# Key factors, directions and the bonus's sums multiplied beside the rates, four and four Fourier steps, four bonus products

## The reference, cut to what matters

```python
w_lora = w0 + einsum("btdr,drc->btdc", tanh(wd), w2)
decay = exp(-exp(-softplus(-w_lora) - 0.5))
a = sigmoid(a0 + einsum("btdr,drc->btdc", ad, a2))      # the rates
kk = normalised(k * k_k)                                # per head of 64
kd = k[:, :, None] * (1 + (a - 1) * k_a)                # key factors, for each direction
bonus = einsum("bthn,btdhn,hn->bth", r, kd, r_k)[..., None] * v    # sums over both directions d
y = fft2(u_fourier, axes=(1, 3)).real                   # the Fourier branch, whose projection is done here too
```

## Time and profile before

| | |
|---|---|
| time, median of 3 runs | 1986.52 us |
| the three runs | 1979.35, 1986.52, 1986.55 us |
| the profiled execution's own time | 1988.64 us |
| its span | 1986.8 us |
| mean granted TensorE clock | 0.953 of full speed |

### The profile page before, as it was taken

The page is one execution under the profiler, slowest core; times in us unless marked ns, Lnnn a source line. Parts: engine busy times, 40 slices in busy tenths (PEclk is TensorE's granted clock), DMA queues, the critical chain, the costliest instruction groups (busy, mean ns, idle before and its releaser), DMA issues. The chain is left out here.

```text
span 1986.8 us, 27840 instructions
## 1 busy us (share of the span) xinstructions
PE 1802.9 (91%) x11850; PEld 1063.5 (54%) x11850; DVE 977.0 (49%) x1621; ACT 389.8 (20%) x710; POOL 163.9 (8%) x218
## 2 busy tenths in 40 slices
PE   7999888888999999999999999899979889888777
PEld 3544467774444444388887888764444223333322
DVE  1773675553188988953279788743041010001013
ACT  4223442432111011110120111451131000000001
POOL 0000007710000000000011111100000000000000
PEclk9999987999999999999998999899979998888999
DMA  9461033114322121332268332302639999999995
GB/s 361 153 248 61 16 79 94 29 35 151 125 85 82 66 85 66 127 115 88 93 241 304 115 97 85 118 17 71 273 130 400 426 426 426 425 427 426 425 426 224
DMA packets 79648, 379.67 MB, mean 191 GB/s; under 512 B 34224, under 2 KB 37296, under 8 KB 53408
## 3 DMA queue, kind: packets, MB, share of 16 engines
q1 hardware_dynamic: 69664, 349.83, 45.3%
q0 software_dynamic: 7104, 26.68, 3.7%
q10 hardware_dynamic: 2752, 1.31, 0.2%
HBM read 363.83 MB, written 19.92 MB: 193 GB/s over the span
## 5 line engine op out<-in xcount | busy, mean ns | idle before, releaser
L3351 PE MATMUL psum<-mem 128*64 128x512 f32 x1504 | 357.9, 632 | 38.5 <-DMA mem<-in_w_upe 13.8
L2074 PE MATMUL psum<-mem 128*128 128x512 f32 x704 | 302.9, 591 | 1.0 <-ACT mem L379 1.0
L3351 PEld LDWEIGHTS psum<-mem 128*64 128x64 f32 x1504 | 118.9, 144 | 256.8 <-issue 252.5
L2183 DVE SCALAR_TENSOR_TENSOR mem<-mem 128x512 f32<-128x512 f32 x352 | 237.0, 746 | 0.0
L2074 PEld LDWEIGHTS psum<-mem 128*128 128x128 f32 x704 | 132.9, 189 | 170.6 <-issue 169.4
L2425 PE MATMUL psum<-mem 128*128 128x256 f32 x896 | 199.9, 385 | 5.3 <-DVE mem L2606 4.8
L2425 PEld LDWEIGHTS psum<-mem 128*128 128x128 f32 x896 | 171.7, 192 | 33.4 <-DVE mem L2606 4.5
L1605 PE MATMUL psum<-mem 128*128 128x256 f32 x616 | 139.8, 387 | 2.3 <-DVE mem L1587 1.1
L3413 DVE TENSOR_TENSOR mem<-mem,psum 128x512 f32<-128x512 f32 x16 | 11.0, 688 | 251.9 <-issue 221.3
L1605 PEld LDWEIGHTS psum<-mem 128*128 128x128 f32 x616 | 118.5, 194 | 22.5 <-issue 4.9
L699 PE MATMUL psum<-mem 128*128 128x512 f32 (+1 forms) x336 | 119.0, 513 | 0.0
(11 more groups left out here) (394 smaller groups left out, 2229.2 us busy)
## 6 DMA issues: line engine op xcount, KB each, us to landing
mem<-in_w_upe SPq DMA_DIRECT2D x31, 2048.0 KB, 29.0
mem<-in_w_gate SPq DMA_DIRECT2D x30, 2048.0 KB, 31.9
mem<-in_w_downe SPq DMA_DIRECT2D x29, 2048.0 KB, 32.5
mem<-in_ada SPq DMA_DIRECT2D x32, 1024.0 KB, 6.4
mem<-in_w_up SPq DMA_DIRECT2D x22, 1024.0 KB, 4.8
mem<-in_ada POOLq DMA_DIRECT2D x16, 1024.0 KB, 5.5
mem<-in_w_in_g SPq DMA_DIRECT2D x12, 1024.0 KB, 5.0
mem<-in_w_down SPq DMA_DIRECT2D x16, 704.0 KB, 4.4
```

Of the source, the lines that this page charges most:

```text
L2074: last = pe.matmul(k.bank[2 * (m % 3) + h2][:, :], w[:, kt, h2], h[:, kt], start=kt == 0, stop=kt == KD - 1)
L2183: ins = dve.scalar_tensor_tensor(out=a, in0=src, scalar=w, in1=a, op0=MUL, op1=ADD)
L3351: last = pe.matmul(bank[halves[h], :], xs[:, kt, halves[h]], pair[h][0][:, kt, cols], start=kt == 0, stop=kt == tiles - 1, skip_group_chec ...
```

## The change

ScalarE scales the rates directly behind the sigmoids of each tile and writes into `K` (its place in memory no longer holds weights or sums of the modulation by then: `acc` and `late_w` have changed places). VectorE makes the key factors and the directions there, in place, in a loop of its own ahead of the loop over units. In that loop it also adds the two directions' key factors and multiplies the sum by `r_k` and `r`, once for each tile, so that there are four products for the bonus in four places (`prods`) and TensorE's `bonus` is one product that isn't accumulated. Four Fourier steps stand between the rates, and four in the loop over units. ScalarE does one exponential of a single column (`warm`) behind the rates. In VectorE's loop over units A, R, K and B are left, and the products with `v` come in units 2, 4, 5 and 6.

```diff
--- before.py
+++ after.py
@@ -624,14 +624,13 @@
     acc, rows = mod_places
     sig = ring(0, 6144).rearrange("p (t d c) -> p t d c", t=6, d=2)
     fourier_in = ring(4096, 2048).rearrange("p (c t) -> p c t", c=KC)
-    upto0, inv_at, scaled0, scaled1, prod = temps
+    upto0, inv_at, prods = temps
     squares = inv_at.rearrange("p (n w) -> p n w", n=2)
-    root, inverse = prod[:, 0:W4], prod[:, W4:2 * W4]
+    root, inverse = prods[0][:, 0:W4], prods[0][:, W4:2 * W4]
     e_upto = [x.rearrange("p (c t) -> p c t", t=CHUNK + 1) for x in (upto0, ring(6144, 780))]
     e_inv = [inv_at[:, ALL * i:ALL * i + ALL] for i in range(2)]
-    kd = [scaled0, scaled1]
     omka = k.small[:, 0:4]
-    late_w = late_weights.rearrange("p (j w) -> p j w", j=KD)[:, :, 0:CH]
+    late_w = late_weights.rearrange("p (j w) -> p j w", j=KD)
     chunks = lambda x: x.rearrange("p (c t) -> p c t", t=CHUNK)
     quarters = lambda x: x.rearrange("p (j w) -> p j w", j=4)
     of_chunks = lambda x: slice(x.start // CHUNK, x.stop // CHUNK)
@@ -644,7 +643,7 @@
         "summed", "copied", "padded", "tap0", "tap1", "conv", "mod_acc", "mod_summed", "mod_rows", "mod_turned", "mod_added", "landed",
         "late_landed", "fourier_mm", "fourier",
         "one_minus", "raw", "square", "length", "root", "inverse", "spread", "kk", "sig_mm", "sig", "a_mm", "a", "ones", "sum",
-        "e_upto", "decay", "e_inv", "scale", "a_done", "r_done", "kd", "prod", "k_done", "kk_a", "b_done", "bonus_mm", "bonus")}
+        "e_upto", "decay", "e_inv", "scale", "a_done", "r_done", "kd", "both", "prod", "warm", "k_done", "kk_a", "b_done", "bonus_mm", "bonus")}
     mod_step = [k.sem("first_mod_step"), 0]
     units = [(ct, d) for ct in range(KC) for d in range(2)]
     n_conv = sum(len(c) for c in convs.values())
@@ -757,12 +756,11 @@
                                      skip_group_check=True)
                 last.then_inc(s["sum"], 1)
 
-            def bonus(n):
-                ct, d = units[n]
-                pe.wait_ge(s["prod"], n + 1)
-                if ct >= 2 and d == 0:
+            def bonus(ct):
+                pe.wait_ge(s["prod"], ct + 1)
+                if ct >= 2:
                     pe.wait_ge(s["bonus"], ct - 1)
-                pe.matmul(k.bank[6 + ct % 2][:, :], k.c("head_ones"), prod, start=d == 0, stop=d == 1,
+                pe.matmul(k.bank[6 + ct % 2][:, :], k.c("head_ones"), prods[ct], start=True, stop=True,
                           skip_group_check=True).then_inc(s["bonus_mm"], 1)
 
             start.tensor(pe, part_of_tile)
@@ -791,19 +789,19 @@
             rates(0)
             pe.wait_ge(s["mod_added"], 2)
             pe.wait_ge(s["late_landed"], 16)
-            fourier(0)
-            rates(1)
-            fourier(1)
-            rates(2)
-            rates(3)
+            for ct in range(KC):
+                if ct:
+                    rates(ct)
+                fourier(ct)
             pe.wait_ge(s["a"], 8)
             sum_logs(0)
             for n in range(8):
                 if n < 7:
                     sum_logs(n + 1)
-                if n < 6:
-                    fourier(n + 2)
-                bonus(n)
+                if n < 4:
+                    fourier(n + 4)
+                if n in (1, 2, 4, 5):
+                    bonus((1, 2, 4, 5).index(n))
 
         @block.scalar
         def _(act):
@@ -822,6 +820,9 @@
                 act.wait_ge(s["a_mm"], ct + 1)
                 for d in range(2):
                     act.activation(B[:, d, ct], a_banks[d], ACT.Sigmoid, bias=k.v("a0", 4 * d + ct)).then_inc(s["a"], 1)
+                act.wait_ge(s["a"], 2 * ct + 2)
+                for d in range(2):
+                    act.activation(K[:, d, ct], B[:, d, ct], ACT.Identity, bias=omka[:, ct:ct + 1], scale=k.v("k_a", ct)).then_inc(s["scale"], 1)
 
             start.scalar(act)
             for i, m in enumerate(order):
@@ -852,9 +853,10 @@
             for t in range(2, 6):
                 take_logs(t)
             act.wait_ge(s["mod_turned"], 1)
+            act.wait_ge(s["one_minus"], 1)
             for ct in range(KC):
                 take_rates(ct)
-            act.wait_ge(s["one_minus"], 1)
+            act.activation(k.small[:, 62:63], k.v("zero"), ACT.Exp).then_inc(s["warm"], 1)
             act.wait_ge(s["ones"], 2)
             for n, (ct, d) in enumerate(units):
                 act.wait_ge(s["sum"], n + 1)
@@ -864,7 +866,6 @@
                 if n >= 2:
                     act.wait_ge(s["b_done"], n - 1)
                 act.activation(e_inv[n % 2], sums, ACT.Exp, scale=-DECAY_SCALE).then_inc(s["e_inv"], 1)
-                act.activation(kd[n % 2], B[:, d, ct], ACT.Identity, bias=omka[:, ct:ct + 1], scale=k.v("k_a", ct)).then_inc(s["scale"], 1)
                 act.wait_ge(s["e_upto"], n + 1)
                 act.activation(chunk_decay[:, :, 4 * d + ct], e_upto[n % 2][:, :, CHUNK], ACT.Copy).then_inc(s["decay"], 1)
             act.wait_ge(s["fourier_mm"], 8)
@@ -874,7 +875,7 @@
         @block.vector
         def _(dve):
             def bonus(ct):
-                dve.wait_ge(s["bonus_mm"], 2 * ct + 2)
+                dve.wait_ge(s["bonus_mm"], ct + 1)
                 dve.tensor_tensor(bonus_v[:, ct], k.bank[6 + ct % 2][:, :], vf[:, ct, CTX:ALL], MUL).then_inc(s["bonus"], 1)
 
             start.vector(dve)
@@ -883,6 +884,8 @@
             dve.tensor_scalar(omka, k.v("k_a", 0, 4), -1.0, 1.0, MUL, ADD).then_inc(s["one_minus"], 1)
             slots = 0
             for i, m in enumerate(order):
+                if i == 7:
+                    dve.wait_ge(s["conv"], 8)
                 for j in range(slots, slots + (2 if i == 7 else 1)):
                     mod_slot(k, dve, "ada1", 8 + j, k.silu[0], acc[:, 256 * j:256 * j + 256], 0, mod_step, s["mod_acc"])
                 slots += 2 if i == 7 else 1
@@ -913,7 +916,21 @@
             dve.wait_ge(s["kk"], KC)
             dve.wait_ge(s["conv"], n_conv)
             for n, (ct, d) in enumerate(units):
-                t2 = kd[n % 2]
+                dve.wait_ge(s["scale"], n + 1)
+                for x in stretches(d):
+                    ins = dve.tensor_tensor(K[:, d, ct, x], K[:, d, ct, x], in_time(d, kf[:, ct, x]), MUL)
+                ins.then_inc(s["kd"], 1)
+                for x in stretches(d):
+                    ins = dve.tensor_tensor(B[:, d, ct, x], B[:, d, ct, x], in_time(d, kk[:, ct, x]), MUL)
+                ins.then_inc(s["kk_a"], 1)
+                if d:
+                    dve.wait_ge(s["kd"], n + 1)
+                    dve.tensor_tensor(prods[ct], K[:, 0, ct, CTX:ALL], in_time(1, K[:, 1, ct, CTX:ALL]), ADD).then_inc(s["both"], 1)
+                    dve.wait_ge(s["both"], ct + 1)
+                    dve.scalar_tensor_tensor(out=prods[ct], in0=prods[ct], scalar=k.v("r_k", ct), in1=r[:, ct],
+                                             op0=MUL, op1=MUL).then_inc(s["prod"], 1)
+            dve.wait_ge(s["kk_a"], 8)
+            for n, (ct, d) in enumerate(units):
                 dve.wait_ge(s["e_upto"], n + 1)
                 dve.wait_ge(s["fourier_mm"], n + 1)
                 for x in stretches(d):
@@ -922,25 +939,13 @@
                 dve.wait_ge(s["decay"], n)
                 dve.tensor_tensor(chunks(R[:, d, ct]), chunks(in_time(d, r[:, ct])), e_upto[n % 2][:, CTX // CHUNK:, 1:CHUNK + 1],
                                   MUL).then_inc(s["r_done"], 1)
-                dve.wait_ge(s["scale"], n + 1)
-                for x in stretches(d):
-                    ins = dve.tensor_tensor(t2[:, x], t2[:, x], in_time(d, kf[:, ct, x]), MUL)
-                ins.then_inc(s["kd"], 1)
-                for x in stretches(d):
-                    ins = dve.tensor_tensor(B[:, d, ct, x], B[:, d, ct, x], in_time(d, kk[:, ct, x]), MUL)
-                ins.then_inc(s["kk_a"], 1)
-                dve.wait_ge(s["kd"], n + 1)
-                if n:
-                    dve.wait_ge(s["bonus_mm"], n)
-                dve.scalar_tensor_tensor(out=prod, in0=in_time(d, t2[:, CTX:ALL]), scalar=k.v("r_k", ct), in1=r[:, ct],
-                                         op0=MUL, op1=MUL).then_inc(s["prod"], 1)
+                dve.wait_ge(s["both"], ct + 1)
                 dve.wait_ge(s["e_inv"], n + 1)
-                dve.tensor_tensor(K[:, d, ct], t2, e_inv[n % 2], MUL).then_inc(s["k_done"], 1)
-                dve.wait_ge(s["kk_a"], n + 1)
+                dve.tensor_tensor(K[:, d, ct], K[:, d, ct], e_inv[n % 2], MUL).then_inc(s["k_done"], 1)
                 dve.tensor_tensor(B[:, d, ct], B[:, d, ct], e_inv[n % 2], MUL).then_inc(s["b_done"], 1)
-                if d == 0 and ct:
-                    bonus(ct - 1)
-            bonus(KC - 1)
+                if n in (2, 4, 5, 6):
+                    dve.wait_ge(s["a_done"], n)
+                    bonus((2, 4, 5, 6).index(n))
 
 
 def solve_blocks(eng, x, n, tmp, step, count):
@@ -2270,9 +2275,9 @@
     r_dram = nc.dram_tensor("scan_r", [P, KC, SEQ], F32, kind="Internal").ap()
```

(6 more changed lines are left out.)

## The result

The changed kernel took 1967.91 us, median of six runs (1964.47 to 1972.45). Six runs of the kernel before, the three that were known and three new ones, have a median of 1980.58 us (1973.68 to 1986.55). The ratio is 0.9938, with a 95% interval of 0.9915 to 0.9962: 0.62% less, or 12.3 us. A second series of the unchanged pair gave 0.9946 (0.9926 to 0.9967), or 10.7 us. These ratios are estimated from all the runs and are not exactly those of the medians, which differ by 12.7 and 12.8 us.

The account below looks back on a forecast made before the run. VectorE was taken to set the loop's end, with TensorE close behind. 263.55 - 251.8 = 11.8 us, less 0.5, gave 11.3: 1977.3 against the profiled execution, 1975.2 on the median's scale; 80% range 1970 to 1985.

Parts of the forecast that it names:

- The sum for the stage: From rates to the end of the loop over units: end at 251.8 instead of 263.55, a gain of 11.8 us.
- the last scale of the fourth pair: ScalarE's scaling of the rates behind the sigmoids: said to land at 213.6 us, VectorE done with all eight factors at 218.6.
- TensorE's chain: Sums, Fourier steps and bonus products in the loop, said to set the pace: 22.3 us from 217.5 to 239.85.
- The deduction of 0.5 us for a colder start of the scan: TensorE idles from 246.0 to 252.1 and starts the scan at 1.2 GHz; 0.5 us taken off the 11.8 us gain.
- some 3 us of low clock: At the scan's start: bound on how far the low-clock phase may differ, at most 1.7 us of time.
- so on the scale of the median 1975.2: Last step: 1977.3 against the profiled execution, which lies 2.1 us above the three-run median 1986.52, gives 1975.2, 0.57% less.
- (a): The forecast itself: loop paced by TensorE, end near 251.8, all passed on; 1971.5 to 1978.5 us; chance 0.56.
- (b): TensorE's clock drops after the gap ahead of `sum_logs(1)`, costing 1.8 us; gain 7.8, time 1978.7; chance 0.22.
- (c): The gain doesn't reach the end: a later stage waits for something whose time doesn't move; about 1986; chance 0.10.
- (d): Slower: TensorE's clock stays at 1.2 GHz through the loop; all 22.3 us affected would give 1997; chance 0.04.
- (e): More than forecast: early Fourier steps at 3.44 and scan start no colder, 12.6 us, or noise; below 1971.5; chance 0.08.
- its clause on noise: The alternative cause given for a time below 1971.5 us: noise in the same direction; no size or chance of its own.

Follow-up runs that it names:

- bonus in the gap: The changed kernel with TensorE's first two bonus products moved between sum 0 and sum 1; 1965.03 us, ratio to the kernel before 0.9928.
- factors only: The changed kernel with the Fourier steps where they were before (two between the rates, six in the loop); ratio to the kernel before 0.9960.
- the delay: The changed kernel with 18 more 128x512 additions on VectorE at the end of the stage; 1981.42 us, ratio to the kernel before 1.0005.
- Fourier steps and early exponential only: The kernel before with four Fourier steps between the rates, four in the loop, and the early exponential; ratio to the kernel before 1.0010.

## Why the prediction was right in its ratio and wrong in its time

*What was right.* The sum for the stage. It said 11.8 us, with the end at 251.8; the profiles show 11.70, and VectorE's last product ends 58.0 us behind the rates (253.49 - 195.49), which is 251.8 - 193.84. Point by point: VectorE is busy from 200.07 - 195.49 = 4.58 us behind the rates (4.5 said), the four blocks take 5.0, the loop starts at 24.8 (24.8 said), TensorE has no gap up to sum 0 and one of 1.72 behind it (1.6 said), sum 5 starts at 44.6 (44.5 from the chain), units 3, 4 and 5 wait for the exponential, and the addition that the trace of before didn't show takes 0.69. (The 213.6 us that the working gives for "the last scale of the fourth pair" is the first of that pair; its later sums use it rightly.) The total fell by 0.62 and 0.54% in two series, against 0.57% said. That TensorE's chain is the pace was shown from both sides: 1.72 us taken from it came back as 1.72, and 1.21 put on it as 1.21. The deduction of 0.5 us for a colder start of the scan stands on weaker ground. The first 256 matmuls of the scan took 10.00 us against 9.29, and 10.29 against 9.45 in the second pair, so 0.7 and 0.8 us more. But behind the same idle time of 5.85 us they took 8.97 with the bonus in the gap, less than before, so that from one execution or version to the next it comes out either way. No row shows the bound of "some 3 us of low clock" and 1.7 us that the working names; the profiles show 8.97 to 10.29 us for these matmuls.

*What was wrong.* The time itself: 1967.91 us lies 2.1 us below the range of 1970 to 1985. The step that failed is the last of the sum, "so on the scale of the median 1975.2", and with it the range's lower end. The median of 1986.52 was that of three runs which spread over 7.2 us; with three more it is 1980.58, 5.9 lower, and later series gave 1978.87 to 1981.00. The same gain taken from 1980.58 is 1969.3. That is still below 1970; the last 1.4 us are gain beyond the forecast (12.7 between the medians against 11.3), of which the stage's 11.70 gives 0.4. The spread was quoted in the working, but the range reached only 5.2 us below the forecast (and 9.8 above it), while the base alone was 5.9 too high. Two of the three runs of before, and its profile at 1988.64, were on the long side; the one of 1979.35 was the typical one. The trace shows where that lay: 1722.9 us from the scan to the end, against 1710.7 to 1717.1 in ten other profiles. Beside its repetition (1712.2), half of the excess had arisen by the first matmul of L2425, 789.8 us behind the scan's start against 784.3, and nearly all by that of L3351, 1232.0 against 1222.0. The granted clock goes with it: 0.90 against 1.00 in the 50 us that begin 1000 us behind the scan's start, and over the whole span 0.953, the lowest of the eleven (the others 0.955 to 0.960). So at least part of it is the clock. Why one execution is granted less than another was not tried and stays open.

*The rivals.* (a) was right in its mechanism, and the measured time lies below its band. (b) needed the clock to fall after the gap ahead of `sum_logs(1)`: it didn't at 1.72 us, but it did at 2.94 (without the early exponential), at a price of 1.68 us, near the 1.8 that was named, and it didn't at 3.29 (factors only). So the line `warm`, whose only priced effect was the load of 1.28 us, was worth 2.9 in the stage: in that execution the longer wait also cost the clock. The rule of the Trainium skill ("TensorE: Matmul & The Clock Gate", A second HAM failure mode), that small idle times between groups make the clock swing, fits the wait of 2.94 us here, and not those of 0.74, 1.72 and 3.29. (c) is refuted by the delay. (d) didn't come: the clock over 216 to 253.5 was 0.98. (e) is the rival in whose band, below 1971.5, the measured 1967.91 lies, and it had a chance of 0.08. Its mechanism didn't come: the first three Fourier steps between the rates took 3.63 us to the next start and not 3.44, and the scan's start was colder and not equal. What came is its clause on noise, by the base.

## What to carry to other kernels

When one engine is relieved, write down the chain of the next one instruction by instruction: here it gave the new end within 0.1 us. An edit that gains nothing by itself (more Fourier steps early) can pay once the pace has changed hands. Measure such a stage by the distance between two fixed instructions within one profile, not by totals. A forecast of an absolute time needs room on both sides for the median of few runs, here 6 us for three. A ratio against runs made beside the changed kernel carries less of it, though not nothing (here 0.9915 to 0.9962).

## What the runs showed of the hardware

A binary operation of GpSimd on 128x768 operands and one of VectorE on two operands in SBUF didn't run side by side: VectorE's took 2.01 to 2.30 us instead of 0.69 to 1.02 and ended 0.5 to 0.9 us behind GpSimd's, and the GpSimd operation that started behind VectorE's took 2.56 instead of 1.81. The Trainium skill ("SBUF — State Buffer", SBUF: two separate sides) describes this as an exclusive lock, held for a whole instruction by whichever starts first; the rows agree.

A wait of TensorE of 1.72 us behind 20 us of full work left its clock at 2.4 GHz. One of 2.94 us at the same place was followed by 5 us with a mean clock of 0.74, that is, partly at 1.2 GHz, and cost 1.68 us more than the wait itself. The length of the wait doesn't decide it alone: behind 3.29 us (factors only) and 2.78 us (Fourier steps and early exponential only, ahead of 244.89) the next sum took 1.61 and 1.50 us, at full clock, while behind 2.96 us in both profiles of the kernel before it took 2.39 and 1.85. What else decides it was not tried.

The ACT_TABLE_LOAD ahead of the exponentials took 1.28 us in all eleven profiles, and the rows show no drain ahead of it or behind it, whether it followed an activation by 0.01 us (the change) or a wait (without the early exponential).
